# Three RMSNorm sums of squares on TensorE: from one f32 product with ones to two fp32r products of a split sum

## The chip, the cores and the metric

One core of a Trainium2 chip runs the whole program in one launch. The metric is the device time of that launch in microseconds (us), smaller is better. The kernel before takes 797.4 us (median of 3 runs, 797.38 to 797.59).

## The reference, cut to what matters

Two decoder layers over 256 tokens of 1024 channels, all in float32. A layer normalises x, projects it into four token mixers and a set of gates, merges them, adds the result to x, normalises again and runs a SwiGLU feed-forward part. The norms are

```
def rms_norm(x, g):
    xf = x.astype(jnp.float32)
    y = xf * lax.rsqrt(jnp.mean(xf * xf, axis=-1, keepdims=True) + EPS)
    return (y * g.astype(jnp.float32)).astype(x.dtype)
...
        hn = rms_norm(x, norm_ffn_g[l])
        gu = hn @ w_ffn_in[l]
        x = x + (jax.nn.silu(gu[..., :FF_DIM]) * gu[..., FF_DIM:]) @ w_ffn_out[l]
```

with D_MODEL 1024, SEQ 256, DEPTH 2 and FF_DIM 2816. There are two such norms in each layer and a last one behind both.

## The kernel before, in words

**Layout.** Activations stand transposed: channels on the 128 partitions, 8 blocks of them, 256 tokens along the free side. `x_res` holds x so. A weight block is 128x2048 numbers of f32, called a unit here; each layer has 69 units, numbered u = 0 to 68. Every unit is loaded by a DMA into one of three `raw` slots (SyncE issues it). ScalarE (ACT) rounds it to `w_hi` (fp32r, line 648), VectorE (DVE) subtracts to get the rest `w_lo` (line 1400, `split`), and TensorE (PE) then runs three products for each pair of blocks: hi*hi, hi*lo, lo*hi (lines 974 to 976). A unit is 48 such products of 256 columns. PE waits for the whole `w_lo` of a unit before its first product (`weights`, the semaphore `lo_ready`).

**Order of work.** Each engine's program is written out by hand in one fixed order; nothing plans it at run time. Units 0 to 10 are the input projection, 11 to 22 and 28 to 31 the gates, 23 to 27 the branch projections, 32 to 35 the output projection, 36 to 68 the feed-forward part in triples: gate part G, up part U, down part O. Unit 36 is G0, 37 U0, 38 G1, 39 U1, 40 O0, 41 G2, 42 U2, 43 O1. ACT and DVE split a unit two or three units ahead of PE. In the feed-forward part they also work on what PE has finished: DVE scales G by the norm (`scaled`, line 1460), ACT takes the silu (line 831), DVE multiplies by the norm again and by U (lines 1683, 1686), ACT rounds (line 648, `ff_hi`), DVE subtracts (line 1691, `ff_lo`), and PE uses that in O.

**The norms.** The gains are multiplied into the activations, and the factor 1/rms is applied to the results of the projections, so PE doesn't wait for it. ACT squares x (line 667), DVE adds the blocks pairwise (`square_sum`, lines 1430 and 1432) to one 128x256 tile `sq[:, 0, :]`, and signals `ssum_ready`. PE (`norm_stat`) multiplies a 128x128 matrix of ones with that tile, in plain f32 (line 1094): this adds over the partitions and leaves the sum in every partition of a PSUM bank. DVE (`norm_scale`) turns it to 1/rms with lines 1440 and 1383 to 1394 into `rms_b`. The function `link` makes an instruction raise a semaphore, for which DVE then waits before it goes on. This form (`spread_sum`) is used for three of the four norms inside the layers: the second of layer 0, the first and the second of layer 1. The first of layer 0 uses lines 1097 to 1100 and the final norm another way.

**What stands around them.** In the feed-forward norm of each layer PE runs `norm_stat` between products of unit 36. On DVE, line 1432 is followed by the split of unit 38, then by `norm_scale`, by the scaling of G0 (line 1460), the split of unit 39, lines 1683 and 1686, 1691, the split of unit 40, and so on with one split for each unit. In the first norm of layer 1, PE runs `norm_stat` between units 1 and 2, and DVE has the splits of units 2 and 3 between line 1432 and `norm_scale`.

Of the kernel before, what the change touches and what calls it, by code (L numbers as in the profile page):

```python
# [28 lines left out]
ALU = mybir.AluOpType  # L29
ACT = mybir.ActivationFunctionType  # L30
AX = mybir.AxisListType
F32 = mybir.dt.float32
F32R = mybir.dt.float32r
# [3 lines left out]
P = 128  # L37
# [106 lines left out]
N_ROWS = 102  # L144
FFN_GAINS = 32

DVE_CHAIN = 141
POOL_CHAIN_PER_LAYER = 8
TAIL_LINKS = 3

# [3 lines left out]
def spread_sum(l, n):  # L154

    return (l, n) != (0, 0)
# [6 lines left out]
def build(nc, T, out, inv_freq, inv_count):  # L163
    L, D, IN_DIM = T["w_in"].shape
    S = T["x"].shape[1]
# [8 lines left out]
    with ExitStack() as ctx:  # L174
        def sb(name, shape, dt=F32):
            return ctx.enter_context(nc.sbuf_tensor(name, shape, dt))

        def sem(name):
            return ctx.enter_context(nc.semaphore(name))
# [7 lines left out]
        sq = sb("sq", [P, KT, S])  # L187
# [7 lines left out]
        y_hi = sb("y_hi", [P, 10, S], F32R)  # L195
        y_lo = sb("y_lo", [P, 10, S], F32R)
# [50 lines left out]
        wsT = sb("wsT", [P, 4, P])  # L247

        ident = sb("ident", [P, P])
        ones = sb("ones", [P, P])  # L250
        zeros = sb("zeros", [P, P], BF16)
        causal = sb("causal", [P, P])
        angles = sb("angles", [P, 2, S])
# [16 lines left out]
        bank = [banks[:, b, :] for b in range(8)]  # L270
# [16 lines left out]
        ssum_ready = sem("ssum_ready")  # L287
# [66 lines left out]
        pre_const = sem("pre_const")  # L354
# [27 lines left out]

        def kview(t):
            return t[:, :].rearrange("p (k n) -> p k n", n=UC)

        def low(b):
            return bank[b][:, :].rearrange("p (f s) -> p f s", f=2)
# [23 lines left out]
        def load_quarter(queue, u, i):  # L411
            c0, ks = W_IN_UNITS[u][1], slice(2 * i, 2 * i + 2)
            queue.dma_start(kview(raw[u])[:, ks, :],
                            T["w_in"][0].rearrange("(k p) n -> p k n", p=P)[:, ks, c0:c0 + UC])\
                .then_inc(quarter_in[u][i] if i < 3 else raw_full[u], 16)
# [30 lines left out]
        def _(sp):  # L446
# [40 lines left out]
            for h, landed in enumerate((half_in, raw_full[2])):  # L487
                ks = slice(4 * h, 4 * h + 4)
                sp.dma_start(kview(raw[2])[:, ks, :], w_rows[:, ks, c0:c0 + UC]).then_inc(landed, 16)
            c0 = W_IN_UNITS[3][1]  # L490
            for i in range(4):
                ks = slice(2 * i, 2 * i + 2)
                if i < 3:
                    sp.wait_ge(quarter_lo[0], i + 1)
                else:
                    sp.dma_start(pos_i, T["positions"].to_broadcast([P, S])).then_inc(pos_in, 16)
                    sp.dma_start(ifreq[:, :], inv_freq).then_inc(ifreq_in, 16)
                    sp.wait_ge(lo_ready[0], 2)
                    sp.sem_inc(raw_claimed, 1)
                sp.dma_start(kview(raw[0])[:, ks, :], w_rows[:, ks, c0:c0 + UC])\  # L500
                    .then_inc(unit3_in if i < 3 else raw_full[0], 16)
# [50 lines left out]
        def _(pool):  # L552
# [2 lines left out]
            pool.wait_ge(pre_const, 2)  # L555
            nc.gpsimd.affine_select(out=ident[:, :], in_=ident[:, :], compare_op=ALU.not_equal, fill=1.0,
                                    base=0, pattern=[[-1, P]], channel_multiplier=1).then_inc(pre_const, 1)
            nc.gpsimd.memset(ones[:, :], 1.0).then_inc(pre_const, 1)
            nc.gpsimd.memset(causal[:, :], 0.0)
            nc.gpsimd.memset(conv_h[:, :, :], 0.0)  # L560
            nc.gpsimd.memset(pool_w[:, :, :], 0.0)
# [14 lines left out]
            n = [0]  # L576
# [19 lines left out]
            for l in range(L):  # L596
# [28 lines left out]
                for i in range(8):  # L625
                    dp = i % 4

                    b, which = (4 + dp, "C") if i < 4 else (dp, "B")
# [342 lines left out]
        def _(pe):  # L971
# [9 lines left out]
            def bank_wait(l, b, what):  # L981
                pe.wait_ge(bank_free[b], free_at(l, b, what))
# [105 lines left out]
            def norm_stat(l, n):  # L1088

                b, what = (7, "stat1") if n == 0 else (4, "stat2")  # L1090
                bank_wait(l, b, what)
                pe.wait_ge(ssum_ready, l * 2 + (n + 1))
                if spread_sum(l, n):
                    nc.tensor.matmul(bank[b][:, 0:S], ones[:, :], sq[:, 0, :], start=True, stop=True)\
                        .then_inc(stat_done, 1)
                    return
                for t in range(TT):
                    last = nc.tensor.matmul(bank[b][:, t:t + 1], sq[:, 0, t * P:t * P + P], ones[:, 0:1],
                                            start=True, stop=True)
                last.then_inc(stat_done, 1)  # L1100
# [19 lines left out]
            def misc(l, u):  # L1120
# [8 lines left out]
                if u == 1 + (l == 0):  # L1129
                    norm_stat(l, 0)  # L1130
# [163 lines left out]
            for l in range(L):  # L1294
# [41 lines left out]
                pe.wait_ge(act_lo_ready, l * 12 + (8 + 2 + 1))  # L1336
                unit_pair(l, U_FFN, 0, (4, 5))
                norm_stat(l, 1)
                pe.wait_ge(act_lo_ready, l * 12 + (8 + 3 + 1))
                unit_pair(l, U_FFN, 0, (6, 7)).then_inc(w_used[g], 1)  # L1340
# [22 lines left out]
        def _(dve):  # L1363
            dve.sem_inc(lo_ready[0], 1)
            dve.sem_inc(params_free, 1)
            V = nc.vector
            n = [0]
            pre = [0]

            def link(l, ins):  # L1370

                if l is None:
                    pre[0] += 1
                    ins.then_inc(tail_chain, 1)
                    dve.wait_ge(tail_chain, pre[0])
                else:
                    n[0] += 1
                    ins.then_inc(dve_chain, 1)
                    dve.wait_ge(dve_chain, n[0])
# [47 lines left out]
            def square_sum(l, n, i):  # L1427

                dve.wait_ge(sq_done, l * 8 + (4 * n + i + 1))
                link(l, V.tensor_tensor(sq[:, 0:2, :], sq[:, 0:2, :], sq[:, 2 * i:2 * i + 2, :], ALU.add))  # L1430
                if i == 3:
                    V.tensor_tensor(sq[:, 0, :], sq[:, 0, :], sq[:, 1, :], ALU.add).then_inc(ssum_ready, 1)

            def norm_scale(l, n):

                b, what = (7, "stat1") if n == 0 else (4, "stat2")
                dve.wait_ge(stat_done, l * 2 + (n + 1))
                if spread_sum(l, n):
                    v, tmp, bits = sq[:, 2, :], sq[:, 3, :], sq[:, 4, :].bitcast(I32)
                    V.tensor_scalar(v, bank[b][:, 0:S], 1.0 / D, EPS, ALU.mult, ALU.add).then_inc(bank_free[b], 1)  # L1440
                    dve.wait_ge(bank_free[b], free_at(l, b, what, True))
                    rsqrt(l, rms_b[:, 0, :], v, tmp, bits)
                    if n == 0:

                        dve.sem_inc(bank_free[6], 1)
                        own = diag[:, :, :]
                        link(l, V.tensor_tensor(own, rms_b[:, 0, :].rearrange("p (t s) -> p t s", t=TT),
                                                ident[:, :].unsqueeze(1).to_broadcast([P, TT, P]), ALU.mult))
                        V.tensor_reduce(rms_t[:, 0:2], own, AX.X, ALU.add).then_inc(diag_ready, 1)
                    return  # L1450
                V.tensor_scalar(st[:, 0:2], bank[b][:, 0:2], 1.0 / D, EPS, ALU.mult, ALU.add).then_inc(bank_free[b], 1)
                dve.wait_ge(bank_free[b], free_at(l, b, what, True))
                rsqrt(l, rms_t[:, 0:2], st[:, 0:2], st[:, 4:6], ist[:, 0:2])
                for t in range(TT):
                    last = V.tensor_scalar(diag[:, t, :], ident[:, :], rms_t[:, t:t + 1], None, ALU.mult)
                last.then_inc(diag_ready, 1)
# [157 lines left out]
            def merge(l, u):  # L1614
# [34 lines left out]
                if u == U_WO + 3:  # L1649
                    dve.wait_ge(tile_done, l * 2 + 2)  # L1650
                    x_update(l, 1, 2)
                    split(l, u + 2)
                    unit_done(l, u)
                    x_update(l, 1, 3)
                    xg_lo(l, 1, 2)
                    xg_lo(l, 1, 3)
                    for i in range(1, 4):
                        square_sum(l, 1, i)
# [29 lines left out]
            def ffn_lo(l, even, j):  # L1688
                e = 0 if even else 1
                dve.wait_ge(ffhi_ready, l * FF_STEPS + (j + 1))  # L1690
                V.tensor_tensor(ff_lo[:, e, :, :], ff_a, ff_hi[:, e, :, :].bitcast(F32), ALU.subtract)\
                    .then_inc(fflo_ready, 1)
# [109 lines left out]
            for i in range(1, 4):  # L1802
                square_sum(0, 0, i)

            for l in range(L):
                if l > 0:
                    split(l, 0)
                    for i in range(4):
                        y_wait(l, i)
                        x_update(l, 0, i)  # L1810
                        if i >= 1:
                            xg_lo(l, 0, i - 1)
                    xg_lo(l, 0, 3)
                    split(l, 1)
                    for i in range(1, 4):
                        square_sum(l, 0, i)
                    split(l, 2)
# [48 lines left out]
                ffn_lo(l, True, FF_STEPS - 1)  # L1866
            assert n[0] == DVE_CHAIN, n[0]

# [75 lines left out]
```

## Time and profile before

| what | value |
|---|---|
| median of 3 runs | 797.4 us |
| the profiled execution's own time | 797.46 us |
| its span, first to last instruction | 795.7 us |
| TensorE busy | 788.1 us, 99% |
| VectorE busy | 618.3 us, 78% |
| ScalarE busy | 436.6 us, 55% |
| GpSimd busy | 146.8 us, 18% |
| mean granted TensorE clock | 0.998 |

The span is what the trace covers; 1.8 us of the execution's time lie around it. Times in the trace count from the start of the span. Matmuls overlap in the trace (one is shown with 0.28 us, the next starts 0.11 us later), so starts, not durations, tell the pace of TensorE.

### The profile page before, as it was taken

Reading aid. Unit: us, or ns where it says so; the run is one execution under the profiler, and the core shown is the slowest. Engines: PE = TensorE matmul, PEld = TensorE weight load, DVE = VectorE, ACT = ScalarE, POOL = GpSimd, SP = SyncE. Lnnn points to the kernel's source line nnn. Section 1 sums busy time; section 2 is a strip of 40 time slices with the busy share of each in tenths; the row PEclk is TensorE's granted clock in tenths of the full one; section 3 lists DMA queues with packets and bytes.
Section 4 is the critical chain, followed back from the end, with each engine's and each line's share of the span. In section 5 each row is a group of like instructions: output and inputs, shape, how many; then the busy total and the mean of one; then the engine's idle time right before and its main releaser. Section 6 shows DMA issues by size and latency. Waiting matters only on the chain.

```text
span 795.7 us, 15715 instructions
## 1 busy us (share of the span) xinstructions
PE 788.1 (99%) x6567; PEld 765.4 (96%) x6567; DVE 618.3 (78%) x761; ACT 436.6 (55%) x568; POOL 146.8 (18%) x148
## 2 busy tenths in 40 slices
PE   8999999999999999999999999999999999999997
PEld 8999999999999999999999999999999999999996
DVE  6899999776886766575698899988678767676764
ACT  6766887544654353434465678765356444434434
POOL 2415763074000000000000466513300000000000
PEclk9999999999999999999999999999999999999999
DMA  9975555456645666646568555544646465656541
GB/s 296 306 242 170 182 172 177 159 170 234 219 144 184 208 207 209 209 163 211 170 201 266 159 168 185 180 160 159 212 159 212 160 204 181 218 195 205 185 159 53
DMA packets 118187, 152.23 MB, mean 191 GB/s; under 512 B 3904, under 2 KB 101778, under 8 KB 118128
## 3 DMA queue, kind: packets, MB, share of 16 engines
q1 hardware_dynamic: 116592, 149.30, 57.7%
q0 software_dynamic: 1360, 1.82, 0.8%
q8 instruction: 43, 0.70, 0.4%
q10 hardware_dynamic: 176, 0.27, 0.1%
q14 instruction: 16, 0.13, 0.0%
HBM read 148.23 MB, written 1.05 MB: 188 GB/s over the span
## 4 chain that ended last, share of the span: by engine, by line
PE 99%; DMA 0%; DVE 0%; ACT 0%; issue 0%; DVEq 0%; ACTq 0%
PE bank L974 28%; PE bank L975 28%; PE bank L976 28%; PE bank L1062 3%; PE bank L1064 3%; PE bank L1065 3%; PE bank L1036 1%; PE bank L1035 1%; PE bank L1034 1%; PE bank L1196 1%; PE bank L1176 1%; PE bank L1022 0%; PE bank L1021 0%; PE bank L1023 0%; PE bank L1152 0%; PE bank L1148 0%
## 5 line engine op out<-in xcount | busy, mean ns | idle before, releaser
L974 PE MATMUL bank<-act,w_hi 128*128 128x256 f32 x1472 | 408.5, 278 | 1.0 <-DVE w_lo L1752 1.0
L975 PE MATMUL bank<-act,w_hi 128*128 128x256 f32 x1472 | 406.6, 276 | 0.0
L976 PE MATMUL bank<-act,w_lo 128*128 128x256 f32 x1472 | 406.6, 276 | 0.0
L1400 DVE TENSOR_TENSOR w_lo<-raw,w_hi 128x2048 fp32r<-128x2048 f32 x135 | 315.4, 2338 | 101.9 <-ACT w_hi L648 100.9
L648 ACT ACTIVATE w_hi<-raw 128x2048 fp32r<-128x2048 f32 (+3 forms) x146 | 265.2, 1824 | 133.4 <-PE bank L976 105.7
L974 PEld LDWEIGHTS bank<-act,w_hi 128*128 128x128 f32 x1472 | 276.4, 188 | 2.2 <-issue 1.7
L975 PEld LDWEIGHTS bank<-act,w_hi 128*128 128x128 f32 x1472 | 276.4, 188 | 0.5
L976 PEld LDWEIGHTS bank<-act,w_lo 128*128 128x128 f32 x1472 | 276.4, 188 | 0.0
L974 PE MATMUL bank<-y_hi,w_hi 128*128 128x256 f32 x288 | 79.7, 277 | 0.0
L976 PE MATMUL bank<-y_hi,w_lo 128*128 128x256 f32 x288 | 79.5, 276 | 0.0
L975 PE MATMUL bank<-y_lo,w_hi 128*128 128x256 f32 x288 | 79.5, 276 | 0.0
L831 ACT ACTIVATE qk<-qk 128x512 f32<-128x512 f32 x22 | 13.9, 633 | 87.9 <-DVE qk L1460 87.9
L648 ACT ACTIVATE ff_hi<-qk 128x512 fp32r<-128x512 f32 x22 | 13.9, 633 | 81.0 <-DVE qk L1686 81.0
L589 POOL TENSOR_TENSOR conv_a<-gates,par 128x256 f32<-128x256 f32 x2 | 3.4, 1710 | 277.2 <-ACT gates L826 277.2
L975 PEld LDWEIGHTS bank<-y_lo,w_hi 128*128 128x128 f32 x288 | 54.1, 188 | 0.0
L974 PEld LDWEIGHTS bank<-y_hi,w_hi 128*128 128x128 f32 x288 | 54.1, 188 | 0.0
L976 PEld LDWEIGHTS bank<-y_hi,w_lo 128*128 128x128 f32 x288 | 54.1, 188 | 0.0
L975 PE MATMUL bank<-ff_lo,w_hi 128*128 128x256 f32 x176 | 48.7, 276 | 0.0
L976 PE MATMUL bank<-ff_hi,w_lo 128*128 128x256 f32 x176 | 48.6, 276 | 0.0
L974 PE MATMUL bank<-ff_hi,w_hi 128*128 128x256 f32 x176 | 48.6, 276 | 0.0
L593 POOL TENSOR_TENSOR conv_a<-conv_a,gates 128x256 f32<-128x256 f32 x30 | 38.4, 1281 | 24.4 <-ACT gates L826 21.5
L631 POOL TENSOR_TENSOR gates<-gates,qk 128x512 f32<-128x512 f32 x16 | 28.4, 1814 | 68.6 <-DVE qk L1612 68.6
(248 smaller groups left out, 996.0 us busy)
## 6 DMA issues: line engine op xcount, KB each, us to landing
raw<-in_w_ffn_in SPq DMA_DIRECT2D x44, 1024.0 KB, 5.0
raw<-in_w_gate SPq DMA_DIRECT2D x32, 1024.0 KB, 5.3
raw<-in_w_ffn_out SPq DMA_DIRECT2D x22, 1024.0 KB, 4.8
raw<-in_w_in SPq DMA_DIRECT2D x18, 1024.0 KB, 6.7
raw<-in_w_o SPq DMA_DIRECT2D x8, 1024.0 KB, 5.0
raw<-in_w_proj_b SPq DMA_DIRECT2D x4, 1024.0 KB, 4.8
raw<-in_w_in SPq DMA_DIRECT2D x12, 256.0 KB, 5.9
gates<-qk SPq DMA_DIRECT2D x32, 64.0 KB, 5.7
```

What stands on the lines that cost most here:

```text
L593: ins = nc.gpsimd.tensor_tensor(conv_a[:, 1, :], conv_a[:, 1, :], tmp, ALU.add)
L631: nc.gpsimd.tensor_tensor(m, m, mtmp[:, i % 2, :], ALU.add).then_inc(madd_done, 1)
L648: return nc.scalar.activation(o, i, ACT.Copy)
L831: nc.scalar.activation(ff_g, ff_g, ACT.Silu).then_inc(silu_done, 1)
L974: nc.tensor.matmul(o, whi, ahi, start=first, stop=False, skip_group_check=skip)
L975: nc.tensor.matmul(o, whi, alo, start=False, stop=False, skip_group_check=skip)
L976: return nc.tensor.matmul(o, wlo, ahi, start=False, stop=last, skip_group_check=skip)
L1034: nc.tensor.matmul(o, act_hi[:, kk, ts], hi[:, k, :], start=(kk == 0), stop=False)
L1062: nc.tensor.matmul(o, y, hi[:, k, cs], start=first and k == 0, stop=False, skip_group_check=True)
L1064: nc.tensor.matmul(o, y, lo[:, k, cs], start=False, stop=False, skip_group_check=True)
L1065: last = nc.tensor.matmul(o, in_lo[:, k, ts], hi[:, k, cs], start=False, stop=last_k and k == 1, skip_group_check=True)
L1400: V.tensor_tensor(lo, raw[slot][:, :], hi.bitcast(F32), ALU.subtract).then_inc(lo_ready[slot], 1)
```

## The change

The matrix of ones is declared as fp32r, and read as f32 where it was used before. At the three norms of the spread form, DVE copies the summed tile to an fp32r tile `sum_hi` (the copy rounds), subtracts it from the sum to get `sum_lo`, and only then signals PE. Both tiles lie in block 9 of `y_hi` and `y_lo`. Line 1432's instruction and the copy are linked, so DVE waits for each. PE runs two products in fp32r that accumulate in the same bank, in place of one in f32.

```diff
-DVE_CHAIN = 141
+DVE_CHAIN = 147
...
-        ones = sb("ones", [P, P])
+        ones_r = sb("ones_r", [P, P], F32R)
+        ones = ones_r[:, :].bitcast(F32)
...
+        sum_hi, sum_lo = y_hi[:, 9, :], y_lo[:, 9, :]
...
-            nc.gpsimd.memset(ones[:, :], 1.0).then_inc(pre_const, 1)
+            nc.gpsimd.memset(ones_r[:, :].bitcast(F32), 1.0).then_inc(pre_const, 1)
...
                 if spread_sum(l, n):
-                    nc.tensor.matmul(bank[b][:, 0:S], ones[:, :], sq[:, 0, :], start=True, stop=True)\
+                    nc.tensor.matmul(bank[b][:, 0:S], ones_r[:, :], sum_hi, start=True, stop=False)
+                    nc.tensor.matmul(bank[b][:, 0:S], ones_r[:, :], sum_lo, start=False, stop=True)\
                         .then_inc(stat_done, 1)
...
-                if i == 3:
+                if i == 3 and not spread_sum(l, n):
                     V.tensor_tensor(sq[:, 0, :], sq[:, 0, :], sq[:, 1, :], ALU.add).then_inc(ssum_ready, 1)
+                elif i == 3:
+                    link(l, V.tensor_tensor(sq[:, 0, :], sq[:, 0, :], sq[:, 1, :], ALU.add))
+                    link(l, V.tensor_copy(sum_hi, sq[:, 0, :]))
+                    V.tensor_tensor(sum_lo, sq[:, 0, :], sum_hi.bitcast(F32), ALU.subtract).then_inc(ssum_ready, 1)
```

## Rows read from the trace of the kernel before

**Rows 1.** The page: busy us, share of the span, number of instructions.
```profile
PE 788.1 (99%) x6567; PEld 765.4 (96%) x6567; DVE 618.3 (78%) x761; ACT 436.6 (55%) x568; POOL 146.8 (18%) x148
```

**Rows 2.** The page: the chain that ended last, by engine.
```profile
PE 99%; DMA 0%; DVE 0%; ACT 0%; issue 0%; DVEq 0%; ACTq 0%
```

**Rows 3.** Timeline of PE, layer 0: start us, us, engine line op operands, count.
```profile
220.12 0.28 PE L976 MATMUL bank<-act,w_lo 128*128 128x256 f32 x1
...
226.58 0.28 PE L976 MATMUL bank<-act,w_lo 128*128 128x256 f32 x1
226.70 0.59 PE L1094 MATMUL bank<-sq,ones 128*128 128x256 f32 x2
226.94 0.47 PE L974 MATMUL bank<-act,w_hi 128*128 128x256 f32 x1
227.24 0.28 PE L975 MATMUL bank<-act,w_hi 128*128 128x256 f32 x1
```

**Rows 4.** Timeline of DVE around the sum in layer 0.
```profile
224.98 0.42 DVE L1432 TENSOR_TENSOR sq<-sq 128x256 f32<-128x256 f32 x1
225.33 2.29 DVE L1400 TENSOR_TENSOR w_lo<-raw,w_hi 128x2048 fp32r<-128x2048 f32 x1
227.53 0.42 DVE L1440 TENSOR_SCALAR sq<-bank 128x256 f32<-128x256 f32 x1
227.98 0.29 DVE L1383 TENSOR_SCALAR sq<-sq 128x256 int32<-128x256 int32 x1
228.31 0.30 DVE L1384 TENSOR_SCALAR rms_b<-sq 128x256 int32<-128x256 int32 x1
...
230.94 0.29 DVE L1392 TENSOR_SCALAR sq<-rms_b 128x256 f32<-128x256 f32 x1
231.15 0.42 DVE L1393 SCALAR_TENSOR_TENSOR sq<-sq 128x256 f32<-128x256 f32 x1
```

**Rows 5.** Timeline of DVE, a copy of another 128x256 tile at the start.
```profile
30.23 0.29 DVE L1779 CAST gates<-gates 128x256 f32<-128x256 int32 x1
```

**Rows 6.** Timeline of DVE, layer 0, splits of units 41 and 42.
```profile
244.35 2.29 DVE L1400 TENSOR_TENSOR w_lo<-raw,w_hi 128x2048 fp32r<-128x2048 f32 x1 [2.40 <-ACT w_hi L648]
...
250.55 2.29 DVE L1400 TENSOR_TENSOR w_lo<-raw,w_hi 128x2048 fp32r<-128x2048 f32 x1 [2.28 <-ACT w_hi L648]
```

**Rows 7.** Timeline of ACT, layer 0, between the sum and unit 42.
```profile
241.88 0.63 ACT L831 ACTIVATE qk<-qk 128x512 f32<-128x512 f32 x1 [3.06 <-DVE qk L1460]
242.41 1.90 ACT L648 ACTIVATE w_hi<-raw 128x2048 fp32r<-128x2048 f32 x1
...
248.07 0.63 ACT L648 ACTIVATE ff_hi<-qk 128x512 fp32r<-128x512 f32 x1 [3.75 <-DVE qk L1686]
248.61 3.72 ACT L648 ACTIVATE w_hi<-raw 128x2048 fp32r<-128x2048 f32 x2
```

**Rows 8.** Timeline of PE's weight loads, layer 0, the first of unit 42.
```profile
252.91 0.19 PEld L974 LDWEIGHTS bank<-act,w_hi 128*128 128x128 f32 x1
```

**Rows 9.** Timeline of DVE, layer 1, the sum and the split of unit 42.
```profile
615.17 0.43 DVE L1432 TENSOR_TENSOR sq<-sq 128x256 f32<-128x256 f32 x1
...
640.70 2.29 DVE L1400 TENSOR_TENSOR w_lo<-raw,w_hi 128x2048 fp32r<-128x2048 f32 x1 [2.04 <-ACT w_hi L648]
```

**Rows 10.** Timeline of PE's weight loads, layer 1, the first of unit 42.
```profile
643.07 0.19 PEld L974 LDWEIGHTS bank<-act,w_hi 128*128 128x128 f32 x1
```

**Rows 11.** Timeline of DVE at the start, two splits of 128x512 merged.
```profile
9.89 1.28 DVE L1729 TENSOR_TENSOR w_lo<-raw,w_hi 128x512 fp32r<-128x512 f32 x2
```

**Rows 12.** Timeline of PE's weight loads at the start, the one that waits for it.
```profile
10.69 0.19 PEld L974 LDWEIGHTS bank<-act,w_hi 128*128 128x128 f32 x1 [0.20 <-issue]
```

**Rows 13.** Timeline of DVE, layer 1, first norm.
```profile
407.62 4.49 DVE L1400 TENSOR_TENSOR w_lo<-raw,w_hi 128x2048 fp32r<-128x2048 f32 x2
...
430.27 2.29 DVE L1400 TENSOR_TENSOR w_lo<-raw,w_hi 128x2048 fp32r<-128x2048 f32 x1 [1.34 <-ACT w_hi L648]
```

**Rows 14.** Timeline of PE, layer 1, first norm.
```profile
411.08 0.59 PE L1094 MATMUL bank<-sq,ones 128*128 128x256 f32 x2
```

## The prediction, written before the changed kernel was run

> **What bounds the kernel now.** Read the busy times first: PE is busy 99% of the span, DVE 78%, ACT 55% [rows 1]. Then the chain that ended last: it is PE for 99% [rows 2]. So anything taken off PE counts, and anything put on DVE counts only where PE then waits for it. That second question can't be answered from shares; it needs the timelines of the engines beside each other, from each of the three sums to the place where DVE's results reach PE with the least time to spare.
>
> The pace of PE: the starts of L976 at 220.12 and 226.58 are 57 products apart, 6.46 / 57 = 0.1133 us for each [rows 3]. A unit of 48 takes 5.44 us.
>
> The least time to spare is at unit 42, the up part U2 of the first feed-forward triples. DVE makes its w_lo at 250.55, ready at 250.55 + 2.29 = 252.84 [rows 6]; PE's first weight load of that unit starts at 252.91 [rows 8], 0.07 us later, with no idle time noted. Layer 1 is the same: 640.70 + 2.29 = 642.99 [rows 9] and 643.07 [rows 10], 0.08 us. That PE's start is its own pace and not a wait: L975 at 227.24 puts the L974 after the sum at 227.13; 36 more products of units 36 and 37 (4.08) and four units of 5.44 give 252.97 for PE and, with weight loads starting 0.11 earlier, 252.86 against 252.91 seen.
>
> **PE's part.** Without the sum, L975 would have started 0.2267 after the L976 at 226.58, at 226.81; it starts at 227.24 [rows 3]. So the f32 product costs 0.43 us (the trace shows it as two instructions). Two fp32r products of 256 columns have the shape of the weights' ones, 0.1133 each: 0.23. The gain is 0.43 - 0.23 = 0.20 to 0.21 us for each of the three, I take 0.21. Bounds: nothing if the new pair went at the old one's pace, 0.21 if at the neighbours'. The first term, were DVE's work hidden: 3 x 0.21 = 0.63 us.
>
> **DVE's part.** Before, line 1432 starts at 224.98 and what is behind it at 225.33, 0.35 later. After, there are three instructions:
> - line 1432 with a link. The pair L1440, L1383 shows what a link costs an instruction of 0.42: the next starts 0.45 later [rows 4].
> - the copy with a link. No copy of f32 to fp32r is in the trace. The nearest row is the CAST of 128x256 at 0.29 [rows 5], and single-input instructions of this size on SBUF take 0.29 too, with the next linked one 0.33 later (227.98 to 228.31) [rows 4]. I take 0.33. Upper bound: the 0.42 of a two-input or PSUM-reading instruction of this size, so 0.45. Lower bound: 0.21, which L1392 needs when nothing waits for it.
> - the subtraction, two inputs, no wait behind it: 0.35, as line 1432 before.
>
> Sum 0.45 + 0.33 + 0.35 = 1.13 against 0.35: everything behind it on DVE moves by D = 0.78 us (bounds 0.66 and 0.90). The sum itself reaches PE later: in layer 0 the subtraction starts at 224.98 + 0.78 = 225.76 and ends, with 0.42, at 226.18; PE comes to the product at 226.70 [rows 3], its weight load 0.11 before. In layer 1's second norm everything lies alike, 615.17 for 224.98 [rows 9]; in its first norm PE comes at 411.08 [rows 14], 3.5 us after DVE has begun what stands behind line 1432, at 407.62 [rows 13]. So no wait at the products themselves.
>
> **What queues behind it.** In the two feed-forward norms DVE goes on with the split of unit 38, norm_scale, G0's scaling and the split of unit 39. From there the chain to unit 42 runs between DVE and ACT only. ACT's rows say so: the silu at 241.88 is released by DVE L1460, ff_hi at 248.07 by DVE L1686 (the triple before has the same pattern), and behind each ACT starts a w_hi at once, at 242.41 and 248.61 [rows 7]; DVE's splits of units 41 and 42 in turn wait for just these w_hi (2.40 and 2.28 idle before them) [rows 6]. The idle time of DVE there is no cover: it waits for ACT, which waited for DVE. No link of this chain is released by PE or a DMA, so D comes through whole, and w_lo of unit 42 is ready at 253.62.
>
> When PE does wait for DVE, it starts later than 0.07 after: at the start of the program the first of two splits of 128x512 ends at about 9.89 + 1.28 - 0.59 = 10.58 (the second starts 0.59 to 0.60 after the first), and the waiting weight load starts at 10.69 [rows 11, 12], 0.11 later. So unit 42 starts at 253.62 + 0.11 = 253.73 in place of 252.91: +0.82 us in layer 0. Whether PE already waits a little at a unit before makes no difference, and PE's 0.21 in this norm is used up in the wait. In layer 1: 642.99 + 0.78 + 0.11 = 643.88 for 643.07, +0.81. Behind unit 42 the delay stays: PE is the bound again and has nothing to catch up with.
>
> In the first norm of layer 1 the splits of units 2 and 3 stand behind the sum. The pair takes 4.49, so unit 2's w_lo is ready at about 407.62 + 2.29 = 409.91, after the change 410.69; PE wants it after its two products, at 411.08 + 0.23 - 0.11 = 411.20 [rows 13, 14]. Half a microsecond is left, and later DVE is idle 1.34 before the split at 430.27, waiting for ACT [rows 13], where the delay ends. Here the 0.21 is kept.
>
> **Sum.** +0.82 + 0.81 - 0.21 = +1.42 us on an execution of 797.46 (795.7 of it in the span; that is 0.06 above the median of 797.4). Predicted: 797.4 + 1.4 = 798.8 us, 0.18% slower.
>
> The Trainium skill, "VectorE: DVE Perf Modes", section "The DRAIN you can't avoid", says that a semaphore after each instruction on DVE costs nothing extra against instructions with none. Here it does: L1383 with a wait behind it holds the next for 0.33, L1392 of the same length without one for 0.21 [rows 4]. By the page the added links are free, which makes a rival below.
>
> **Rivals.** A measurement of this kernel can tell about 0.2%, 1.6 us, from no change.
> - A, the copy or a wait costs more. With a copy at 0.45, D is 0.90: 2 x 0.94 - 0.21 = +1.67, 799.1 us. For it: no row shows a rounding copy. Against: all single-input instructions from SBUF of this size take 0.29. Were PE also slower to start again after a wait, by a further 0.1 at each of the two, 799.3.
> - B, the links cost nothing. Then the spacings are 0.35, 0.21 and 0.35, D = 0.56: 2 x 0.60 - 0.21 = +0.99, 798.4 us. For it the unlinked pair, against it the linked pairs [rows 4].
> - C, the other side: the delay is lost before unit 42, and all three savings are kept, -0.63, 796.8 us. The place would be ACT's w_hi of units 40 to 42: if one of them is really released by a landing DMA or by PE freeing its slot, DVE has that much room. It decides from D: what is left at unit 42 must be under 0.07 us in both layers for the whole 0.63. If x of D is left there, a layer loses x + 0.04, and with the 0.21 of layer 1 the kernel is slower from x = 0.07 on. For it: ACT idles 3.06 and 3.75 us at a time; against it, the releasers named are DVE's [rows 7].
> - D, the change doesn't do what it says: the pair in fp32r takes as long as the f32 product. Then nothing is saved in layer 1's first norm, +1.63, 799.0 us. Against: products of the same shape and format at 0.1133 all around.
>
> **Chances.** The forecast 0.60, its own range 798.5 to 799.1; A 0.13, B 0.08, C 0.12, D 0.02, something not thought of 0.05. Over 799.0 lie all of A but its edge (0.11), the upper part of the forecast (0.13), half of D and most of the unforeseen: 0.28. Under 795.8 lies only a part of the unforeseen: 0.02. Between, the rest: 0.70. The range 797.6 to 799.5 holds the forecast, A, B and D and leaves C out, and a small part of the unforeseen.
>
> **What would show it.** Right: the copy at 0.29 and the split of unit 38 starting 1.13 after line 1432; the first matmul behind the new pair 0.23 later than without it; at unit 42 of both layers PE's weight load 0.1 behind the end of w_lo, and idle time of PE that the page of before doesn't have, some 1 us a layer; all between unit 42 of layer 0 and the first norm of layer 1 shifted by 0.8. Wrong: unit 42 starting within 0.1 us of 252.9 and a kernel under 797.3; a copy of 0.42; PE waiting at the product with ones; or a delay at another place, in the attention part of layer 1.

## The result, and the profile after

The changed kernel takes 799.34 us (median of 15 runs, 798.71 to 800.89) against 797.41 for the kernel before on the same chip: a ratio of 1.0027, 95% interval 1.0019 to 1.0035, so it is slower, clear of noise. Forecast were 798.8 us and, with a chance of 0.70, no change that can be told. The time lies in the range, but the change can be told: the loss is 1.93 us where 1.4 was forecast, and the interval reaches only 0.6 us to either side, where I had taken 1.6 us as the least that can be told.

The page of this first profile, and the chain that ended last:

```profile
PE 790.9 (99%) x6567; PEld 767.6 (96%) x6567; DVE 620.2 (78%) x767; ACT 436.2 (55%) x568; POOL 148.0 (19%) x148
...
PE 88%; DVE 7%; ACT 3%; issue 1%; DVEq 0%; ACTq 0%; POOL 0%; POOLq 0%
```

DVE has six instructions more [rows 1], and the chain, all PE before [rows 2], now goes through DVE and ACT for a tenth of the span (E1's trace gives the same line). Idle time of PE, invisible in a share of 99%, shows here.

That execution took 800.89 us; 1.4 us of it were lost in its first 25 us, where nothing was changed, and the same is seen in other kernels here (last section). So I read the other trace of the same kernel, from the first experiment (799.12 us). DVE and PE at the sum in layer 0, one timeline for each; they answer to [rows 4] and [rows 3]:

```profile
224.88 0.42 DVE L1438 TENSOR_TENSOR sq<-sq 128x256 f32<-128x256 f32 x1
225.33 0.29 DVE L1439 CAST y_hi<-sq 128x256 fp32r<-128x256 f32 x1
225.66 0.43 DVE L1440 TENSOR_TENSOR y_lo<-sq,y_hi 128x256 fp32r<-128x256 f32 x1
226.00 2.28 DVE L1404 TENSOR_TENSOR w_lo<-raw,w_hi 128x2048 fp32r<-128x2048 f32 x1
```
```profile
226.47 0.28 PE L979 MATMUL bank<-act,w_lo 128*128 128x256 f32 x1
226.59 0.28 PE L1097 MATMUL bank<-y_hi,ones_r 128*128 128x256 f32 x1
226.70 0.28 PE L1098 MATMUL bank<-y_lo,ones_r 128*128 128x256 f32 x1
226.81 0.28 PE L977 MATMUL bank<-act,w_hi 128*128 128x256 f32 x1
```

The spacings are 0.45, 0.33 and 0.34: 1.12 where 1.13 was forecast. The copy is a CAST of 0.29. PE takes the two products at its pace and doesn't wait. Then the splits of units 40 and 42 on DVE, and PE's first weight loads of these units [rows 6, 8]:

```profile
240.00 2.29 DVE L1404 TENSOR_TENSOR w_lo<-raw,w_hi 128x2048 fp32r<-128x2048 f32 x1 [1.59 <-ACT w_hi L651]
...
251.60 2.29 DVE L1404 TENSOR_TENSOR w_lo<-raw,w_hi 128x2048 fp32r<-128x2048 f32 x1 [2.28 <-ACT w_hi L651]
```
```profile
242.34 0.19 PEld L977 LDWEIGHTS bank<-ff_hi,w_hi 128*128 128x128 f32 x1 [0.60 <-DVE w_lo L1404]
...
253.95 0.19 PEld L977 LDWEIGHTS bank<-act,w_hi 128*128 128x128 f32 x1 [0.63 <-DVE w_lo L1404]
```

and the same for unit 42 of layer 1 [rows 9, 10]:

```profile
642.37 2.29 DVE L1404 TENSOR_TENSOR w_lo<-raw,w_hi 128x2048 fp32r<-128x2048 f32 x1 [2.05 <-ACT w_hi L651]
```
```profile
644.72 0.19 PEld L977 LDWEIGHTS bank<-act,w_hi 128*128 128x128 f32 x1 [0.59 <-DVE w_lo L1404]
```

PE waits where it was said to, at unit 42 of both layers. It waits at unit 40 too (0.60 us idle above, 0.20 in layer 1), which the forecast left open and which adds nothing: how late unit 42 starts is set by its own w_lo. In layer 0 unit 42 comes 253.95 - 252.91 = 1.04 late; at the sum this execution was 0.11 ahead of the one before (226.59 for 226.70), so layer 0 costs 1.15 us, where 0.82 was forecast. Layer 1: PE comes to the first sum at 412.18 for 411.08 and to the second at 617.77 for 616.88, which is 0.21 less between them, the gain, and to unit 42 at 644.72 for 643.07: 1.65 - 0.89 = 0.76 us, where 0.81 was forecast.

```profile
412.18 0.28 PE L1097 MATMUL bank<-y_hi,ones_r 128*128 128x256 f32 x1
...
617.77 0.28 PE L1097 MATMUL bank<-y_hi,ones_r 128*128 128x256 f32 x1
```
```profile
616.88 0.38 PE L1094 MATMUL bank<-sq,ones 128*128 128x256 f32 x1
```

(The second fence is the kernel before, whose other sum is in [rows 14].) So 1.15 + 0.76 - 0.21 = 1.70 us up to the first weight loads of the two units 42. From sum to sum layer 0 costs (412.18 - 226.59) - (411.08 - 226.70) = 1.21 us, another 0.06, because PE doesn't go on at its full pace behind the wait: in layer 0 its next 13 products start 0.118 us apart instead of 0.113 (in layer 1 only the first few do). From the sum in layer 0 to the end of the span it is 570.81 us for 569.04, a loss of 1.77.

Most of what layer 0 has over the forecast stands in the row of unit 40: ACT's w_hi was done at 237.59 + 1.91 = 239.50, DVE's wait for it ended at 239.58, and the split started at 240.00.

```profile
237.59 1.91 ACT L651 ACTIVATE w_hi<-raw 128x2048 fp32r<-128x2048 f32 x1
```

So the split started 0.41 us behind the end of its wait. Before the change it was 0.05, as the wait ended at 238.90:

```profile
238.95 2.29 DVE L1400 TENSOR_TENSOR w_lo<-raw,w_hi 128x2048 fp32r<-128x2048 f32 x1 [1.22 <-ACT w_hi L648]
```

The idle time there grew from 1.22 to 1.59 us: DVE held back by 0.37 us more with nothing to wait for that the trace shows. I call this the hold. The experiments had to say why.

### The profile page after: what moved, and what is told of

Its sections match the earlier page's. It is cut to its first block, busy times and chain, and to the rows that moved or that the text cites. A ratio compares the mean times of both kernels' runs of the same rounds, so it can differ in the third digit from the quotient of the medians.

```text
span 798.9 us, 15721 instructions
## 1 busy us (share of the span) xinstructions
PE 790.9 (99%) x6567; PEld 767.6 (96%) x6567; DVE 620.2 (78%) x767; ACT 436.2 (55%) x568; POOL 148.0 (19%) x148
## 4 chain that ended last, share of the span: by engine, by line
PE 88%; DVE 7%; ACT 3%; issue 1%; DVEq 0%; ACTq 0%; POOL 0%; POOLq 0%
PE bank L977 25%; PE bank L979 24%; PE bank L978 24%; DVE w_lo L1404 4%; PE bank L1068 2%; PE bank L1067 2%; PE bank L1065 2%; ACT w_hi L651 2%; PE bank L1037 1%; PE bank L1038 1%; PE bank L1039 1%; PE bank L1200 1%; PE bank L1180 1%; DVE sq L1434 1%; PE bank L1024 0%
## 5 line engine op out<-in xcount | busy, mean ns | idle before, releaser
L596 POOL TENSOR_TENSOR conv_a<-conv_a,gates 128x256 f32<-128x256 f32 x30 | 36.7, 1222 | 24.6 <-ACT gates L829 21.7
```

The lines of the kernel that those rows point to most:

```text
L596: ins = nc.gpsimd.tensor_tensor(conv_a[:, 1, :], conv_a[:, 1, :], tmp, ALU.add)
```

## The experiments

All against the kernel before on the same chip. E1 to E4, E5 to E8 and E9 to E12 shared a chip each. The forecasts were counted from 797.4 us. The medians can tell 0.7 us either way. One trace tells more, because the time from the start of the product with ones in layer 0 to the end of the span leaves out the start of the program, where executions of one kernel differ. It is 569.04 us in the kernel before. The last column gives what each kernel has over that. Two traces of the changed kernel (first profile and E1) agree to 0.01 us in it, and so do those of E8 and E11, and E9 and E12 come within 0.02 of the kernel before.

| experiment | median us | kernel before | ratio, 95% interval | forecast us | first sum to end, by trace, us |
|---|---|---|---|---|---|
| E1 again | 799.15 | 797.42 | 1.0020 (1.0011 to 1.0029) | 799.3 | +1.77 |
| E2 one memset ahead | 798.82 | 797.42 | 1.0018 (1.0009 to 1.0028) | 798.9 | +1.36 |
| E3 before, two memsets | 797.99 | 797.42 | 1.0007 (0.9998 to 1.0016) | 797.8 | +0.42 |
| E4 first norm only | 797.33 | 797.42 | 0.9998 (0.9989 to 1.0007) | 797.2 | -0.22 |
| E5 DVE's part only | 799.60 | 797.75 | 1.0021 (1.0011 to 1.0030) | 799.5 | +1.98 |
| E6 PE's part only | 797.55 | 797.75 | 0.9999 (0.9990 to 1.0008) | 796.8 | -0.13 |
| E7 shorter root | 797.23 | 797.75 | 0.9993 (0.9984 to 1.0002) | 796.8 | -0.42 |
| E8 weights first | 797.15 | 797.75 | 0.9992 (0.9983 to 1.0001) | 796.8 | -0.65 |
| E9 before, weights first | 797.47 | 797.42 | 0.9998 (0.9989 to 1.0007) | 797.4 | +0.01 |
| E10 weights first, one product | 796.43 | 797.42 | 0.9987 (0.9978 to 0.9996) | 796.5 | -1.00 |
| E11 weights first again | 796.92 | 797.42 | 0.9994 (0.9985 to 1.0003) | 796.8 | -0.65 |
| E12 before, nine memsets | 797.33, one run | 797.42 | | | +0.01 |

### Where the 0.37 us come from: E1, E2, E3, E12

**E1**, no edit. 

> The changed kernel once more. In its first profile the weight split of unit 40 in layer 0 started 0.41 us after the wait before it was over, with nothing to wait for; before the change 0.05 us. This hold makes the difference between the forecast (+1.4 us) and the measured +1.9. Theory H (the hold belongs to the place in DVE's program: that split is DVE's row number 319 of the trace, counted from 0; the other hold of this size is at row 831, exactly 512 further): the same hold at the same row again, +1.9 us, 799.2 to 799.4. Theory R (the hold was an accident of that one execution): no hold in this profile, and then 0.45 us of the measured difference have no cause in the trace. Both expect +0.8 us from D at unit 42 of layer 1 and -0.2 at the first norm of layer 1.

The hold is there again: 0.41 us between the end of the wait and the split of unit 40, as in the first profile.

**E2** and **E3**, the changed kernel with one and the kernel before with two of

```diff
+            V.memset(spare[:, 0:1], 0.0)
             dve.wait_ge(pre_pe, 1)
```

E2: 

> The changed kernel with one memset of 128x1 more at the head of DVE's program, where DVE idles for 4 us. Every later instruction of DVE moves by one row: the split of unit 40 in layer 0 is row 320, and row 319 is the wait before it, which DVE reaches early. Theory H (place in the program): the hold falls into DVE's idle time, unit 42 of layer 0 comes 0.4 earlier, +1.45 us, 798.9. Theory R (no tie to the place): as the changed kernel, +1.9, 799.3.

E3: 

> The kernel before with two memsets of 128x1 at the head of DVE's program. Its split of unit 40 in layer 0, row 317, becomes row 319. Theory H: the hold of 0.4 us appears there, and as unit 42 has 0.07 us to spare, nearly all of it comes through: +0.35 to +0.4 us, 797.8. Theory R: no change, 797.4, within 0.1.

The split of unit 40 in E2, then in E3, and PE's first load of unit 42 in E3:

```profile
239.73 2.29 DVE L1405 TENSOR_TENSOR w_lo<-raw,w_hi 128x2048 fp32r<-128x2048 f32 x1 [1.22 <-ACT w_hi L652]
```
```profile
240.63 2.29 DVE L1401 TENSOR_TENSOR w_lo<-raw,w_hi 128x2048 fp32r<-128x2048 f32 x1 [1.58 <-ACT w_hi L649]
```
```profile
254.58 0.19 PEld L975 LDWEIGHTS bank<-act,w_hi 128*128 128x128 f32 x1 [0.29 <-DVE w_lo L1401]
```

One tiny instruction, executed 239 us earlier in idle time, takes the hold away (idle 1.22, as before the change), and two bring it into the kernel before (1.58), where PE now waits for unit 42. In E2 PE's weight load of unit 42 comes at 253.67, the sum at 226.69: a loss of 0.77 in layer 0, within 0.01 of that of layer 1 in E1. In E3 unit 42 comes 0.37 later behind the sum than in the kernel before, and the end 0.42. The medians alone couldn't tell it: E1 and E2 differ by 0.33, and E3's +0.57 has an interval that still holds none. The traces do: theory H holds, R falls.

**E12**, the kernel before with nine memsets: 

> The kernel before with nine memsets of 128x1 at the head of DVE's program. It puts a DVE instruction that starts 0.04 us behind a wait (a gated product of the branch merges, row 246) on row 255, and none on rows 319 or 831. If the hold of 0.4 us comes every 64 or 128 rows, it is seen at row 255; if only at 63 + 256 n or 319 + 512 n, nothing is seen, and unit 42 of layer 0 comes as in the kernel before.

(A row is one entry of DVE in the trace, waits included.) No hold at row 255: that product starts 0.04 us behind its wait. Holds were seen at row 319 (first profile, E1, E3, E5) and row 831 (first profile, E1, E5, E8, E11): there the instruction starts 0.40 to 0.41 us behind the end of its wait, on an idle engine. In E8 and E11 the split of unit 40 stands in row 319 too, but DVE is still busy with ff_lo when its wait ends, and nothing is lost. There is a third place. In E8, E10, E11 and E12 row 63 starts 0.46 us behind the end of its wait each time, though it is not the same instruction in E12. In E11 the wait ended at 39.90 and DVE's instruction before was done at 40.13:

```profile
40.36 0.43 DVE L1503 TENSOR_TENSOR cos_r<-cos_r,rms_b 128x256 f32<-128x256 f32 x1 [0.23 <-issue]
```

### Which part costs: E4, E5, E6

**E4**, `square_sum` and `norm_stat` of the change only for n == 0:

```diff
-                if i == 3 and not spread_sum(l, n):
+                if i == 3 and (n == 1 or not spread_sum(l, n)):
```

> The change at the first norm of layer 1 alone; the two feed-forward norms keep the f32 product and the undivided sum. By my steps all that is lost is lost at unit 42 behind the feed-forward norms, and this one keeps PE's 0.21: -0.2 us, 797.2. Rival (the extra DVE work costs something wherever it stands, through the attention part behind it): +0.2 to +0.6, 797.6 to 798.0.

In the trace unit 3 of layer 1 comes 0.22 us earlier against unit 1 than in the kernel before, and it stays so to the end. By the median alone (-0.09) it can't be told from no change. The split of unit 40 has no hold here, as nothing was added ahead of it.

**E5**, the change with the old product:

```diff
-                    nc.tensor.matmul(bank[b][:, 0:S], ones_r[:, :], sum_hi, start=True, stop=False)
-                    nc.tensor.matmul(bank[b][:, 0:S], ones_r[:, :], sum_lo, start=False, stop=True)\
+                    nc.tensor.matmul(bank[b][:, 0:S], ones[:, :], sq[:, 0, :], start=True, stop=True)\
```

> DVE's part alone: the sum is copied, rounded and subtracted as in the change, but PE runs the old f32 product of the undivided sum. By my steps PE's saving counts only in the first norm of layer 1, as it is used up in the wait at unit 42 in the other two: 0.2 us slower than the changed kernel, +2.1 us, 799.5. Rival (PE's saving counts at all three and hides a larger loss): 0.63 slower than the changed kernel, +2.5, 799.9.

+1.85 against +1.73 in E1, and by the traces +1.98 against +1.77: DVE's part alone makes the whole loss, and the faster products give back only the 0.21 of the first norm of layer 1. The hold is there too. In the two feed-forward norms the old product and the new pair cost the same up to unit 42 (1.15 and 0.76 us over the kernel before, in E5 as in E1), so PE's saving there is used up in the waits.

**E6**, no instruction more on DVE (the rest of the edit gives PE the rounded tile twice and halves the factor 1/1024):

```diff
-                    link(l, V.tensor_tensor(sq[:, 0, :], sq[:, 0, :], sq[:, 1, :], ALU.add))
-                    link(l, V.tensor_copy(sum_hi, sq[:, 0, :]))
-                    V.tensor_tensor(sum_lo, sq[:, 0, :], sum_hi.bitcast(F32), ALU.subtract).then_inc(ssum_ready, 1)
+                    V.tensor_tensor(sum_hi, sq[:, 0, :], sq[:, 1, :], ALU.add).then_inc(ssum_ready, 1)
```

> PE's part alone: the last addition of the sum writes the rounded fp32r tile at once, so DVE has no instruction more than before, and PE runs the two fp32r products, both with the rounded tile; the factor 1/1024 is halved. The rest of the sum is left out. By my steps all three savings are kept, nothing is lost: -0.6 us, 796.8. Rival (the fp32r pair is no faster than the f32 product): 0, 797.4.

A miss that teaches: -0.20, not -0.6. The split of unit 42 in layer 0 and PE's first load of that unit:

```profile
250.25 2.29 DVE L1404 TENSOR_TENSOR w_lo<-raw,w_hi 128x2048 fp32r<-128x2048 f32 x1 [2.28 <-ACT w_hi L651]
```
```profile
252.59 0.19 PEld L977 LDWEIGHTS bank<-act,w_hi 128*128 128x128 f32 x1
```

PE starts 0.05 behind the end of w_lo, at 252.54. It came to the sum at 226.38, 0.32 ahead of the kernel before, and to unit 42 also 0.32 ahead: the 0.22 gained at the sum were lost again at unit 42. The chain on DVE and ACT starts before the product and gains nothing by it, and of 0.07 us to spare 0.05 are the least that PE needs. A faster product there is worth at most 0.02 up to unit 42. In layer 0 the slower products behind the wait take even that: from sum to sum E6 loses 0.07.

### Whether unit 42 is the only place: E7, E8, E9, E10, E11

**E7**:

```diff
-                link(l, V.tensor_tensor(tmp, o, o, ALU.mult))
-                link(l, V.tensor_tensor(tmp, tmp, v, ALU.mult))
+                if not short:
+                    link(l, V.tensor_tensor(tmp, o, o, ALU.mult))
+                    link(l, V.tensor_tensor(tmp, tmp, v, ALU.mult))
...
-                    rsqrt(l, rms_b[:, 0, :], v, tmp, bits)
+                    rsqrt(l, rms_b[:, 0, :], v, tmp, bits, short=n == 1)
```

> The changed kernel with two multiplications (0.46 us each) of the second Newton step left out in the two feed-forward norms; it leaves out that part of 1/rms. DVE's chain behind the sum is then 0.92 shorter, against D of 0.78. By my steps unit 42 has 0.2 us to spare again, and all three savings show: -0.6 us, 796.8. Rival (the loss is made somewhere else than in the chain from the norm to unit 42): as the changed kernel, or at most the 0.92 of DVE's busy time less: +1.0 to +1.9, 798.4 to 799.3.

-0.52 by the medians, -0.42 by the trace. With 0.92 us less in the chain the 1.7 us are gone. Not all of that is the shorter chain: the two multiplications left out make up for the two rows added, the split of unit 40 is back in row 317, and the hold is gone with it. In the trace w_lo of unit 42 is still what PE waits for, by less: D - 0.92 = -0.14 is smaller than the 0.22 that PE has gained, so the saving of a feed-forward norm is kept to 0.13 or 0.14 up to unit 42 (0.07 from sum to sum in layer 0) and not whole.

**E8**, one swap on ACT:

```diff
                 split(l, U_FFN + 3)
                 ffn_silu(l, 0, 0)
-                ffn_hi(l, 0, 0)
...
-                def ffn_unit(l, base_u, use0, it, c):
+                def ffn_unit(l, base_u, use0, it, c, hi_first=False):
...
                     split(l, base_u + ahead, use0 + ((base_u + ahead) // RING - base_u // RING))
+                    if hi_first:
+                        ffn_hi(l, 0, 0)
...
-                with act.Fori(0, FF_ITERS) as it:
+                for c in range(6):
+                    ffn_unit(l, U_LOOP, U_LOOP // RING, 0, c, hi_first=c == 0)
+                with act.Fori(1, FF_ITERS) as it:
```

> The changed kernel, whole, with one swap on ACT in each feed-forward part: w_hi of unit 40 is made before ff_hi of the first triple and not behind it, in ACT's 2.96 us of idle time; the first turn of ACT's loop is written out for that. DVE's splits of units 40 to 42 can then start some 1.2 us earlier against PE. By my steps that covers D and the hold: unit 42 doesn't wait in either layer, and all three savings are kept: -0.6 us, 796.8. Rival (another result of the norm than w_lo of unit 42 is late, such as the scaled G0 or ff_lo): the loss stays, +0.8 to +1.9, 798.2 to 799.3.

**E11**, the same again. 

> The whole change with the swap on ACT again, beside the kernel before with the swap on the same chip: -0.65 us against both, 796.8. The trace of its first run had no wait of PE for w_lo in the feed-forward parts and 0.22 less at each of the three sums.

ACT in layer 0, DVE's split of unit 42 and PE's first load of it, in E11:

```profile
234.07 1.91 ACT L651 ACTIVATE w_hi<-raw 128x2048 fp32r<-128x2048 f32 x1
237.13 0.63 ACT L651 ACTIVATE ff_hi<-qk 128x512 fp32r<-128x512 f32 x1 [1.15 <-DVE qk L1697]
```
```profile
250.00 2.29 DVE L1407 TENSOR_TENSOR w_lo<-raw,w_hi 128x2048 fp32r<-128x2048 f32 x1 [2.28 <-ACT w_hi L651]
```
```profile
252.64 0.19 PEld L980 LDWEIGHTS bank<-act,w_hi 128*128 128x128 f32 x1
```

w_hi of unit 40 is rounded in ACT's former idle time. Unit 42 now has 252.64 - 252.29 = 0.35 us to spare, in layer 1 0.34, PE waits for w_lo at no unit of the feed-forward parts, and each of the three sums gives 0.22 in the trace. -0.60 and -0.50 us by the medians, each with an interval that still touches 1; -0.65 by both traces, as forecast.

**E9**, the kernel before with the swap. 

> The kernel before with the swap on ACT of the last experiment (w_hi of unit 40 ahead of ff_hi of the first triple) and nothing of the change. It gives unit 42 some 1.2 us to spare instead of 0.07, but PE doesn't wait there in the kernel before. Theory: 0, 797.4, within 0.1 us. Rival (the swap is worth something by itself): -0.3 or more.

+0.05, by the trace +0.01: the swap is worth nothing by itself, though unit 42 has 1.36 us to spare. So the 0.65 of E8 and E11 are PE's savings.

**E10**, the swap and E6's DVE line with one product instead of two:

```diff
-                    nc.tensor.matmul(bank[b][:, 0:S], ones_r[:, :], sum_hi, start=True, stop=False)
-                    nc.tensor.matmul(bank[b][:, 0:S], ones_r[:, :], sum_lo, start=False, stop=True)\
+                    nc.tensor.matmul(bank[b][:, 0:S], ones_r[:, :], sum_hi, start=True, stop=True)\
```

> The swap on ACT, and at the three norms only the rounded sum in one fp32r product: the last addition writes the fp32r tile itself, so DVE does no more than before, and the part of the sum that rounding takes off is left out. PE saves 0.43 - 0.11 = 0.32 us at each of the three, and with 1.2 us to spare at unit 42 all are kept: -0.95 us, 796.5. Rival (something else stands close behind unit 42's w_lo): between -0.3 and -0.6.

-0.99 us, ratio 0.9987 (0.9978 to 0.9996): the one version whose median is clear of the kernel before, at the price of a sum rounded to fp32r. In the trace each sum gives 0.33.

## Why the prediction was wrong

- **PE's part**: right. 0.22 for each product pair, at the place where it counts.
- **DVE's part**: right. D is 0.78 in the trace of E2 (the split of unit 42 starts at 251.33 for 250.55), forecast 0.78; the copy takes the 0.29 of the nearest row. Rivals A and D fall. So does B: the link on line 1432 costs its 0.1.
- **What queues behind it**: the place was right in both layers (E7 and E8 free it and the loss goes), and D comes through whole. The step that failed is "w_lo of unit 42 is ready at 253.62" as the sum of the old chain and D. The chain had a further term that the change brought in by adding two rows to DVE's program ahead of it: 0.37 us of hold at the split of unit 40 in layer 0. The sum put this at nothing. By the traces of E1 and E2 it costs 0.41 us (1.77 - 1.36). What makes the hold stays open.
- **What a measurement can tell**: wrong as well. I had written that less than 0.2%, 1.6 us, can't be told from no change, and the chance of 0.70 rests on it. The intervals are 0.1% wide to either side. E2, the same kernel without the hold, loses 1.40 us, 0.18%, just what was forecast, and its interval of 1.0009 to 1.0028 still leaves out no change. So the forecast of no change would have failed without the hold too.
- **PE's start behind a wait**: I took 0.11 us from a row of the program's start (the estimate of rival C has it too); at unit 42 it is 0.05 (253.89 to 253.95, 644.66 to 644.72). Up to unit 42 a layer loses 0.75 to 0.78 in E1 and E2, the hold aside, and not 0.82. In layer 0 the slower products behind the wait, which the sum had not, add 0.06 in E1 and 0.03 in E2, so that the 0.82 nearly came out by luck. Terms as measured in E1: 0.77 + 0.37 + 0.06 + 0.77 - 0.22 = 1.75 us, by the trace 1.77; the sum was 1.42, E1's median +1.73, E2's without the hold +1.40 (+1.36 by the trace).
- **Rival C** fell, and its price was wrong: with DVE's work hidden I had all three savings kept, -0.63. E6 shows that two of them are worth at most 0.02 each up to unit 42, as the same 0.07 us that makes D cost its full length leaves no room for PE to be faster. With the room that the swap makes (1.36 us in E9) all three are kept (E8, E11).
- The first measurement, +1.93, has 0.2 us more than E1's, within its interval. Four of its 15 runs are at 800.57 or above, 1 of 15 of the kernel before at 798.9.

## What to carry to other kernels

Before moving work off the engine that is busy 99%, list its waits behind the place of the change, and for each how long the thing waited for had been ready. The smallest of these numbers says how much later the other engines may get at no cost. Where their chain doesn't itself wait for the busy engine, it is also the most that a saving of the busy engine can bring. Here it was 0.07 us against 0.78 added, while ACT idled 3 us beside it. One swap on ACT turned the loss into the gain of 0.65 us that the change was made for.

## What the runs showed of the hardware

A hold of 0.4 us on DVE belongs to a place in its program and not to the instruction: at the split of unit 40 it goes when one instruction is put 239 us ahead of it (E2), and comes in the kernel before with two (E3). A change of a few tenths of a microsecond by "one more instruction" may be only this; the same edit on both kernels tells it apart.

The second is the slow start. PE's weight loads at the start, in the first profile of the changed kernel:

```profile
6.86 0.33 PEld L978 LDWEIGHTS bank<-act,w_hi 128*128 128x128 f32 x1
7.08 0.33 PEld L979 LDWEIGHTS bank<-act,w_lo 128*128 128x128 f32 x1
7.29 0.33 PEld L977 LDWEIGHTS bank<-act,w_hi 128*128 128x128 f32 x1
```

and in E1's trace of the same kernel:

```profile
6.80 0.19 PEld L978 LDWEIGHTS bank<-act,w_hi 128*128 128x128 f32 x1
6.92 0.19 PEld L979 LDWEIGHTS bank<-act,w_lo 128*128 128x128 f32 x1
7.04 0.19 PEld L977 LDWEIGHTS bank<-act,w_hi 128*128 128x128 f32 x1
```

In the first profile they start 0.21 us apart and take 0.33 until 10.4 us, in the other 0.12 and 0.19. The granted clock of that stretch is given as 1.00 in both, but this isn't a reading: the trace's record of the clock has its first entry, the full 2.4 GHz, at 10.40 us in the first profile and at 4.95 in E1, and none before it. In all 14 traces the pace changes where this first entry stands, at 4.2 to 6.0 us in eleven and at 10.2 to 10.4 in three. So the slow stretch lies ahead of the rise to the upper level, and its pace, about half of the other, fits the lower one, 1.2 GHz. The other two late ones are E3 (10.19) and E5 (10.21); in the kernel before it stands at 4.83. It costs 1.3 to 1.4 us. That most runs of the kernel before at 798.7 to 799.1 have it too would fit, as their spans are 797.0 to 797.3 us for 795.7, but none of those was profiled. The Trainium skill, "TensorE: Matmul & The Clock Gate", section "What's actually happening", says that the array starts at the lower level and that the point where it rises differs from run to run of one kernel; the two traces of the changed kernel agree, with 10.40 and 4.95 us.
